# VectorE instead of ScalarE makes the first tap of a causal convolution, and its neighbours in the program change places

## What is computed

```python
h = h + concatenate([y_a, y_b]) @ w_out        # y_a: gMLP heads, y_b: Mamba-2 SSD heads
hid = relu(rmsnorm(h) @ w_ff1)
h = h + (hid * hid) @ w_ff2
h = h + sigmoid(rmsnorm(h) @ w_gate) * (p @ w_ple)
```

```python
out[t] = sum_k w[k] * x[t - 3 + k] + bias      # k = 0..3; w[3] is the tap on the position itself
xbc = silu(out)
```

## Time and profile before

| what | value |
|---|---|
| median of 3 runs | 745.14 us (744.86 to 745.29) |
| the profiled execution, its own time | 745.83 us |
| its span, first to last instruction | 744.1 us |
| TensorE busy | 721.5 us, 97% |
| VectorE busy | 535.4 us, 72% |
| ScalarE busy | 416.1 us, 56% |
| GpSimd busy | 134.6 us, 18% |
| mean granted TensorE clock | 0.992 |

### The profile page before, as it was taken

The page is one execution under the profiler, slowest core; times in us unless marked ns, Lnnn a source line. Parts: engine busy times, 40 slices in busy tenths (PEclk is TensorE's granted clock), DMA queues, the critical chain, the costliest instruction groups (busy, mean ns, idle before and its releaser), DMA issues.

```text
span 744.1 us, 9900 instructions
## 1 busy us (share of the span) xinstructions
PE 721.5 (97%) x3908; PEld 618.4 (83%) x3908; DVE 535.4 (72%) x570; ACT 416.1 (56%) x526; POOL 134.6 (18%) x111
## 2 busy tenths in 40 slices
PE   9999996799999999999999999999999999999996
PEld 7788774588888888888899889998899889988884
DVE  6448883666757655565798995799578966898874
ACT  7734644355448681233757744585355736573875
POOL 1030000555465200001101221111310222020000
PEclk9999999989999999999999999999999999999999
DMA  9922220332342244216677799779987997887311
GB/s 340 316 86 74 69 85 30 113 114 86 124 159 85 80 151 166 85 44 202 159 208 175 192 283 210 185 212 235 239 183 200 211 272 164 243 177 256 114 58 56
DMA packets 53446, 119.83 MB, mean 161 GB/s; under 512 B 5372, under 2 KB 5528, under 8 KB 53400
## 3 DMA queue, kind: packets, MB, share of 16 engines
q1 hardware_dynamic: 40888, 85.60, 33.7%
q0 software_dynamic: 11136, 29.36, 21.6%
q10 hardware_dynamic: 1376, 4.23, 1.9%
HBM read 98.18 MB, written 4.23 MB: 138 GB/s over the span
## 4 chain that ended last, share of the span: by engine, by line
PE 82%; DVE 9%; DMA 3%; ACT 2%; issue 2%; SPq 0%; ACTq 0%; DVEq 0%; POOLq 0%
PE acc L1695 23%; PE acc L1697 23%; PE acc L1696 23%; PE side L1770 2%; PE side L1866 2%; PE side L1696 2%; PE side L1695 2%; PE side L1697 2%; DVE ring_lo L1453 2%; DVE conv L1391 1%; DMA quarter<-quarter 1%; DMA w_raw<-in_w_in 1%; PE side L1833 1%; DVE w_lo L1129 1%; PE side L1873 1%
## 5 line engine op out<-in xcount | busy, mean ns | idle before, releaser
L784 ACT ACTIVATE ring_hi<-quarter 128x1024 fp32r<-128x1024 f32 x112 | 113.5, 1051 | 102.7 <-PE acc L1697 48.8
L1453 DVE TENSOR_TENSOR ring_lo<-quarter,ring_hi 128x1024 fp32r<-128x1024 f32 x112 | 132.9, 1220 | 36.4 <-ACT ring_hi L784 36.1
L1695 PE MATMUL acc<-w_hi,a_hi 128*128 128x512 f32 x256 | 105.3, 411 | 1.7 <-ACT h L933 1.1
L1697 PE MATMUL acc<-w_hi,a_lo 128*128 128x512 f32 x256 | 100.7, 393 | 0.0
L1696 PE MATMUL acc<-w_lo,a_hi 128*128 128x512 f32 x256 | 100.7, 393 | 0.0
L1696 PE MATMUL acc<-xS_lo,ring_hi 128*128 128x256 f32 x256 | 72.4, 283 | 0.0
L655 POOL DMA_DIRECT2D quarter<-in_w_ff x24 | 29.2, 1224 | 238.8 <-DMA quarter<-in_w_ff 238.5
L1695 PEld LDWEIGHTS acc<-w_hi,a_hi 128*128 128x128 f32 x256 | 48.7, 190 | 13.3 <-issue 1.7
L1696 PEld LDWEIGHTS acc<-w_lo,a_hi 128*128 128x128 f32 x256 | 48.7, 190 | 11.2 <-issue 1.7
L1697 PEld LDWEIGHTS acc<-w_hi,a_lo 128*128 128x128 f32 x256 | 48.6, 190 | 10.6
L1697 PE MATMUL acc<-xA_hi,ring_lo 128*128 128x256 f32 x192 | 54.3, 283 | 0.0
(11 more groups left out here) (296 smaller groups left out, 1833.0 us busy)
## 6 DMA issues: line engine op xcount, KB each, us to landing
quarter<-in_w_ff SPq DMA_DIRECT2D x72, 512.0 KB, 6.3
w_raw<-in_w_in SPq DMA_DIRECT2D x32, 512.0 KB, 3.6
quarter<-quarter POOLq DMA_DIRECT2D x32, 512.0 KB, 7.5
quarter<-in_w_ff POOLq DMA_DIRECT2D x24, 512.0 KB, 7.5
w_raw<-in_w_out SPq DMA_DIRECT2D x16, 512.0 KB, 3.3
h<-in_x SPq DMA_DIRECT2D x8, 512.0 KB, 5.7
seg<-cs_dram ACTq DMA_DIRECT2D x8, 512.0 KB, 3.8
w_raw<-in_w_ple_gate SPq DMA_DIRECT2D x8, 512.0 KB, 5.4
```

What stands on the lines that cost most here:

```text
L784: act.activation(ring[n % 3][0][at], quarter[i][at], ACT.Copy).then_inc(form_hi, 1)
L1453: dve.tensor_tensor(lo[at], src, hi[at].bitcast(F32), ALU.subtract).then_inc(form_lo, 1)
L1695: pe.matmul(dst, st[0], mv[0], start=start, stop=False)
L1697: return pe.matmul(dst, st[1], mv[0], start=False, stop=stop)
```

## The change

VectorE makes the first tap itself, out of the PSUM bank: `conv` = (bank times w[3]) times `rstd_row`, ahead of `tmp` (one more VectorE instruction for each of the 12 tiles, one fewer on ScalarE). Tap 1 now waits for `tmp` and the first tap, both of VectorE. TensorE transposes xs tile i in iteration i + 10 instead of i + 9, and ScalarE copies it to `y` in iteration i + 11 instead of i + 10; their side banks move with them, and `csT` moves from side bank 0 to 1. VectorE copies `cs` and `csT` ahead of its wait for the group of that iteration instead of behind it. And ScalarE executes a one-column Gelu ahead of the main loop.

```diff
         for t in range(9, 20):
-            if t < 17:
-                plan.append((("xs", t - 9), (t - 9) % 2))
+            if 10 <= t < 18:
+                plan.append((("xs", t - 10), t % 2))
...
             if t == 16:
-                plan.append(("csT", 0))
+                plan.append(("csT", 1))
...
             act.wait_ge(rstd_ready, NS)
+            act.wait_ge(sqrt_loaded, 1)
+            act.activation(early_rms[:], eps[:], ACT.Gelu).then_inc(gelu_loaded, 1)
...
-                if 10 <= t < 18:
-                    bank = wait_full(act, ("xs", t - 10))
+                if 11 <= t < 19:
+                    bank = wait_full(act, ("xs", t - 11))
...
-                    if i >= 2:
-                        act.wait_ge(silu_done, i - 1)
-                    act.wait_ge(*emptied(b, s))
-                    act.activation(conv[:, i % 2, :], tmp[:, i % 2, :], ACT.Copy, scale=cols[:, 36 + i:37 + i]
-                                   ).then_inc(conv_begun, 1)
                     act.wait_ge(conv_step, 3 * i + 3)
...
+                if t == 16:
+                    bank = wait_full(dve, "decay")
+                    dve.tensor_copy(cs[:], bank[:, 0:NS * R]).then_inc(cs_ready, 1)
+                if t == 17:
+                    bank = wait_full(dve, "csT")
+                    freed(dve.tensor_copy(csT[:], bank[0:NS * R, 0:P]), "csT")
                 if X <= b < U:
                     i = t - 4 * X
                     dve.wait_ge(acc_full, t + 1)
...
                     if i >= 2:
-                        dve.wait_ge(conv_begun, i - 1)
+                        dve.wait_ge(silu_done, i - 1)
                         dve.wait_ge(conv_step, 3 * (i - 1))
+                    dve.scalar_tensor_tensor(conv[:, i % 2, :], acc[:, s, :], cols[:, 36 + i:37 + i], rstd_row,
+                                             ALU.mult, ALU.mult).then_inc(conv_begun, 1)
                     dve.tensor_tensor(tmp[:, i % 2, :], acc[:, s, :], rstd_row, ALU.mult).then_inc(dve_evac, 1)
-                if t == 16:
-                    bank = wait_full(dve, "decay")
-                    dve.tensor_copy(cs[:], bank[:, 0:NS * R]).then_inc(cs_ready, 1)
-                if t == 17:
-                    bank = wait_full(dve, "csT")
-                    freed(dve.tensor_copy(csT[:], bank[0:NS * R, 0:P]), "csT")
...
                     dve.wait_ge(conv_begun, i + 1)
+                    dve.wait_ge(*emptied(b, s))
...
-                if 9 <= t < 17:
-                    i = t - 9
+                if 10 <= t < 18:
+                    i = t - 10
                     pe.wait_ge(silu_done, i + 1)
                     turn(("xs", i), lambda c: xs_t[:, i % 2, c * P:c * P + P])
```

More of the change, by code:

```diff
@@ L229, in build_layer @@
         ones_ready = sem("ones_ready")
+        gelu_loaded = sem("gelu_loaded")
         consts_ready = sem("consts_ready")
@@ L869, in _ @@
                     act.activation(v_rms[:], v_ssq[:], ACT.Sqrt, bias=eps[:], scale=1.0 / P).then_inc(v_rms_ready, 1)
-                if 10 <= t < 18:
-                    bank = wait_full(act, ("xs", t - 10))
-                    if t == 10:
+                if 11 <= t < 19:
+                    bank = wait_full(act, ("xs", t - 11))
+                    if t == 11:
                         act.wait_ge(xa_lo, KT)
                         act.wait_ge(ws_masked, 1)
-                    ins = act.activation(y[:, :, (t - 10) * P:(t - 10) * P + P],
+                    ins = act.activation(y[:, :, (t - 11) * P:(t - 11) * P + P],
                                          bank.rearrange("p (c n) -> p c n", c=NS), ACT.Copy)
-                    freed(ins, ("xs", t - 10))
+                    freed(ins, ("xs", t - 11))
                 if t == 11:
@@ L1089, in _ @@
                 if b:
+                    act.wait_ge(gelu_loaded, 1)
                     act.wait_ge(sqrt_loaded, j + 1)
@@ L1299, in _ @@
                         wait_free(dve, "rstd_row")
+                        wait_free(dve, "cols")
                     if i >= 2:
-                        dve.wait_ge(conv_begun, i - 1)
+                        dve.wait_ge(silu_done, i - 1)
                         dve.wait_ge(conv_step, 3 * (i - 1))
+                    dve.scalar_tensor_tensor(conv[:, i % 2, :], acc[:, s, :], cols[:, 36 + i:37 + i], rstd_row,
+                                             ALU.mult, ALU.mult).then_inc(conv_begun, 1)
                     dve.tensor_tensor(tmp[:, i % 2, :], acc[:, s, :], rstd_row, ALU.mult).then_inc(dve_evac, 1)
-                if t == 16:
-                    bank = wait_full(dve, "decay")
-                    dve.tensor_copy(cs[:], bank[:, 0:NS * R]).then_inc(cs_ready, 1)
-                if t == 17:
-                    bank = wait_full(dve, "csT")
-                    freed(dve.tensor_copy(csT[:], bank[0:NS * R, 0:P]), "csT")
                 if t >= 22 and t % 2 == 0:
```

## The result

The changed kernel takes **749.3 us** (median of 4 runs, 748.9 to 750.5). The medians differ by 4.3 us. The ratio over all runs is 1.0068, with an interval of 1.0054 to 1.0081, which is 5.1 us (4.0 to 6.0): slower by 0.7%. The profiled execution took 749.39 us with a span of 747.7, beside 745.83 and 744.1 before. These two single executions are only 3.6 us apart, since the profiled one of before was slower than its median.

The account below looks back on a forecast made before the run. TensorE, busy 721.5 of 744.1 us, was taken as the bound, VectorE as second limit. Terms 0.2 + 7.9 - 2.7 - 1.7 - 3.7 + 0.4 + 0.6 + 2.4 = +3.4 us gave 748.5 us, range 744.6 to 750.4.

Parts of the forecast that it names:

- start and Gelu: Before the main loop: the added one-column Gelu loads nothing earlier and makes TensorE 0.2 us later.
- sums, start: Cumulative sums wait for side bank 1 until xs tile 5 is copied behind tile 7's SiLU: +7.9 us.
- exponentials, mix bank: TensorE's waits for the exponentials and a mix bank vanish through VectorE's early copies: -2.7 and -3.7 us.
- dip behind the exponentials: The half-speed clock after TensorE's wait for the exponentials goes with that wait: -1.7 us.
- dip behind the sums: Slow TensorE clock after the new 8.5 us wait, the middle of two dips: +2.4 us, bounds 1.7 and 3.4.
- B bank: TensorE's wait ending with tile 10's taps grows from 4.4 to 5.0 us: +0.6, bounds 0 and 1.5.
- xs turn: One xs transpose on TensorE now lies behind the cumulative sums instead of ahead of them: +0.4 us.
- The first tap: On VectorE, 0.61 us per tile, bounds 0.55 and 0.75; tile 7's last tap ends at 112.4 us.
- Rival (b): Cumulative sums find their bank free, so the kernel is faster: 737.9 us, about 742 with half the stall; chance 0.09.
- (a): Clock dips behind TensorE's two long waits come out short: 745.6 us, or 744.6; chance 0.21 shared with (d).
- (d): Nothing measurable changes, stalls being exchanged one for one; same time as (a), with which it shares chance 0.21.
- Rival (c): More VectorE-GpSimd collision, or a dip after iteration 11's wait: 749.4 or 750.2 us, both 751.1; chance 0.11.

Follow-up runs that it names:

- The bank's own run: Changed kernel with the cumulative sums in side bank 0 instead of 1: 742.3 us, ratio 0.9962.
- the copy-ahead run: Changed kernel with ScalarE copying each xs tile out ahead of the same iteration's SiLU, one iteration earlier than before: 741.2 us, ratio 0.9954.
- The run with work in the wait: Changed kernel with 34 extra matmuls, whose result nobody reads, put on TensorE ahead of the cumulative sums: 746.1 us, ratio 1.0024.
- without the Gelu: Changed kernel without the one-column Gelu activation and the waits on it: 750.4 us, ratio 1.0073.
- both undone: Changed kernel with the first tap back on ScalarE and the cumulative sums in side bank 0: 736.6 us, ratio 0.9896.
- with evictions early: Kernel before with early cs and csT copies, plus ScalarE evicting mix heads 6, 7 and B bank 0 ahead of tile 10's SiLU: 736.9 us.
- tap alone: Kernel before with only the first tap moved from ScalarE to VectorE: 748.0 us, ratio 1.0046.

## Why the prediction was right

The forecast was 748.5 us with a range of 744.6 to 750.4, by an exchange of waits; it came out at 749.3, by that exchange. The tap, the long wait and the wait at `dtT` stand in the timelines where the prediction put them, and VectorE shows no idle row between 72 and 112 us. Step by step, as lateness of TensorE against the profile of before:

| step | predicted | measured | from |
|---|---|---|---|
| start and Gelu | +0.2 | +0.7, of which the Gelu 0.1 | 29.90 instead of 29.22 |
| sums, start | +8.1 with the Gelu | +8.6 | 115.33 instead of 106.75 |
| exponentials, mix bank | -2.7, -3.7 | the same | no idle time at either |
| dip behind the exponentials | -1.7 | the same | the wait is gone |
| dip behind the sums | +2.4 | +3.1 | half of the 6.2 us at 0.50, from 115.3 to about 121.5 |
| B bank | +0.6 | +0.8 | 5.18 instead of 4.42 |
| B turn, start, in all | +3.4, with the dip behind it unchanged | +4.4 | 153.03 instead of 148.63 |

The measured terms make 4.4 without the +0.4 that was put down for the xs turn; that one doesn't show.

- **The first tap** was taken at 0.61 us of VectorE's time. Its follower starts 0.66 us later (72.37 and 73.03), and the last tap of tile 7 ends at 113.1 instead of 112.4, which is as much as the late start of 0.7 explains. It lasts 0.74 us, and what it adds, 0.66, is inside the bounds.
- **The sums.** The term that decides was right: the bank, the copy behind the SiLU, and the size, 7.9 us on top of the start. The bank's own run and the copy-ahead run confirm the two halves of the cause: either another bank or another place in ScalarE's list takes the wait down to 2.04 us.
- **The clock** is the term that was mis-sized. I took the middle of two dips, 2.4 us; the part of the dip behind the wait is 6.2 us long, where the dip of the earlier trace rows behind 2.71 us of idle time was 3.4, and it costs 3.1. The run with work in the wait measured 3.2. It was within the bounds, near the upper one. The dip behind the B bank, which the prediction had measured at 3.1, was the better model.
- **The start** is mostly not the Gelu's. ScalarE's rows of after:

```profile
26.70 1.06 ACT L677 ACTIVATE w_hi<-w_raw 128x1024 fp32r<-128x1024 f32 x1 [0.28 <-DMA w_raw<-in_w_in]
...
29.07 0.20 ACT L852 ACTIVATE early_rms<-eps 128x1 f32<-128x1 f32 x1
```

The last rounding ahead of the table load starts at 26.70 us instead of 26.10, since its weights landed later; that is 0.6 of the 0.7. The Gelu starts at 29.07 and its follower at 29.18, so it costs 0.1. Executions differ here by as much as the effect and more: in the version with the sums in their own bank, which has the Gelu, TensorE's wait ends at 28.90, and without the Gelu at 29.36.
- **The later part.** The prediction has the lateness constant behind 160 us. It is +4.4 up to 424 us and +3.6 from 433 us to the end. The 0.8 us are lost by the execution of before within these nine microseconds, in the feed-forward part, where TensorE waited for `fS_lo` from VectorE, the low part of one of its operands:

```profile
426.36 0.50 PE L1695 MATMUL acc<-ring_hi,fS_S_hi 128*128 128x512 f32 x1 [0.16 <-DVE fS_lo L1529]
```

The change touches no instruction there, and whether it is the execution or the change that spared the kernel this wait stays open. Against the profile it hid the excess of the clock and the start, so that the forecast looks better by 0.8 us than its terms are. That is luck. (The prediction read the 468.61 of 472 us as time that TensorE loses there. All but 0.27 of it is time behind its last matmul.)
- **Rival (b)** was priced wrong: 737.9 us if the bank were free. With the bank free the kernel takes 742.3. The bank was not free at once there, the sums still waited 2.04 us. And I counted the tap as nearly free once TensorE no longer waits at the sums. It isn't. VectorE's row of `tmp` for tile 6 and tile 7, first with both undone and then with the sums in their own bank:

```profile
99.13 0.69 DVE L1314 TENSOR_TENSOR tmp<-acc,gain 128x512 f32<-128x512 f32 x1
104.80 0.69 DVE L1314 TENSOR_TENSOR tmp<-acc,gain 128x512 f32<-128x512 f32 x1
```

```profile
103.33 0.68 DVE L1311 TENSOR_TENSOR tmp<-acc,gain 128x512 f32<-128x512 f32 x1
109.65 0.68 DVE L1311 TENSOR_TENSOR tmp<-acc,gain 128x512 f32<-128x512 f32 x1
```

From tile to tile it takes 5.67 us without the tap and 6.32 with it, and by tile 7 VectorE is 4.85 us later. It is the limit there, and TensorE pays for it at `dtT` (1.79) and at the sums (2.04), with a dip behind each. The first dip comes back to VectorE, which has one idle row, 1.60 us of the 4.85:

```profile
87.68 0.75 DVE L1309 SCALAR_TENSOR_TENSOR conv<-acc,cols,gain 128x512 f32<-128x512 f32 x1 [1.60 <-PE acc L1700]
```

The prediction put the 742 that came out to half the stall and short dips, which is another reason.
- **Rivals (a) and (d)** didn't come: both dips are long, 3.1 and 3.0 us lost behind their waits.
- **Rival (c)**, a dip behind the wait at `dtT`, didn't come in the changed kernel, but did in the version with its own bank: the wait of 1.79 us was the same in both. The 1.60 us of VectorE's above are what (c) describes: a dip there makes VectorE wait for TensorE and passes on nearly whole.

## What to carry to other kernels

A change that moves a step to the engine with less work on the page is to be judged by that engine's share in the stage: VectorE is busy for 72% of the span before, but was full where the step went. When steps are moved, ask of every shared buffer who empties it and what stands ahead of that in the emptier's list; a bank held by an instruction behind a wait is held for the whole wait. And try the parts one by one: here one part was worth 8.3 us, two others cost about 7 and 6, and together they read as a small loss.

## What the runs showed of the hardware

**The clock behind a wait.** TensorE's idle time, and the granted clock behind it, in short windows of several runs:

| kernel | wait, us | clock behind it |
|---|---|---|
| changed | 1.79 | 1.00 |
| sums in own bank | 1.79 | 0.51 for 3 us |
| sums in own bank | 2.04 | 0.57 over 4 us |
| copy ahead of the SiLU | 2.04 | 1.00 |
| with evictions early | 2.68 | 0.50 for 5 us |
| tap alone | 2.82 | 1.00 |
| tap alone | 3.36 | 0.50 for 3 us |
| before | 3.73 | 1.00 |
| changed | 8.39 | 0.50 for 6 us |

```profile
108.00:112.00 4.00, 3.31 (x18) 2.85 (x18) 3.95 (x6) 0.63 (x2) 0.00 (x0) 1.00 0.13 17
```

This is the window behind the 2.04 us in the copy-ahead run. Waits of one length end with and without a dip, so the length doesn't decide alone; what else does, no run here tells. Each row is one execution, and executions of one kernel differ too: the 8 runs with the sums in their own bank go from 742.6 us at a mean granted clock of 0.987, the profiled one, to 740.2 us at 0.996. Every wait of TensorE's of over 4 us between 50 and 300 us, in all profiles (4.26 to 8.39 us), had a dip behind it. What of a dip lies behind the wait costs half its length, and work in the wait prevented it both times that it was tried, with 3.2 and 2.0 us won.

The Trainium skill (TensorE: Matmul & The Clock Gate, section "Why this matters for your kernels") gives a rule of thumb of about 3 us as the idle time to stay below. The dips behind 1.79 and 2.04 us show that less can be too much, and the 3.73 us that more can go well.

**GpSimd and VectorE.** Taps, which read two tensors of SBUF, take 2.3 us for three when alone, 5.77 us beside GpSimd's `seg` step, and `w_lo` 3.43 instead of 1.22. The new tap, which reads PSUM, `cols` and `gain`, did not suffer at 149.47, beside another of GpSimd's steps, of 148.96 to 150.45. It is one instance, and not beside a `seg` step:

```profile
149.47 0.74 DVE L1309 SCALAR_TENSOR_TENSOR conv<-acc,cols,gain 128x512 f32<-128x512 f32 x1
...
148.96 1.49 POOL L631 TENSOR_TENSOR y<-y,d_skip 128x512 f32<-128x512 f32 x1
```

The Trainium skill (SBUF — State Buffer, section "SBUF: two separate sides") describes the port pair that the two share as an exclusive lock, taken for a whole instruction when VectorE's has two SBUF inputs. The rows agree in kind. In size they can't be checked so simply: the `seg` step of 3.25 us goes on for 2.33 us beside the taps (143.77 to 146.10) and two shorter steps follow it, while the taps take 3.5 us more than alone.
